# Opening of a decoder-layer kernel: two small loads issued by ScalarE instead of SyncE, and twelve idle products of TensorE split 6 + 8 instead of 8 + 4

## The reference, cut to what matters

```
h = concatenate([meta_tokens, x], axis=1)          # 272 x 2048
xn = rmsnorm(h, norm1_g)                           # h * rsqrt(mean(h*h) + eps) * norm1_g
proj = xn @ w_in                                   # 2048 x (columns of all mixers and gates)
... three token mixers, gated merge, w_o, residual, MLP (w_up, conv, w_down), final rmsnorm
```

## Time and profile before

| | us |
|---|---|
| median of 3 runs | 1773.64 |
| lowest, highest | 1773.37, 1773.96 |
| the profiled execution, its own time | 1775.31 |
| its span (first to last instruction) | 1773.6 |
| TensorE busy in it | 1762.3 (99%) |
| mean granted clock of TensorE | 0.998 |

### The profile page before, as it was taken

How to read it: one execution, slowest core, us unless ns; L and a number is a source line. 1 busy time by engine, 2 the same in 40 slices (tenths; PEclk the granted TensorE clock), 3 DMA queues, 4 the chain that set the end, 5 groups by cost and what they waited for, 6 DMA issues and landing times.

```text
span 1773.6 us, 34047 instructions
## 1 busy us (share of the span) xinstructions
PE 1762.3 (99%) x13517; PEld 1698.4 (96%) x13517; DVE 1133.6 (64%) x1557; ACT 763.9 (43%) x942; POOL 160.3 (9%) x306
## 2 busy tenths in 40 slices
PE   9999999999999999999999999999999999999998
PEld 8999999999999999999999999999999999888886
DVE  6857757677575545555556587777777777544444
ACT  6634444354354444444444444444434343443433
POOL 3030030210300000000000033331000000000000
PEclk9999999999999999999999999999999999999999
DMA  8655556556455565666555566666556555655554
GB/s 229 171 156 158 169 153 172 157 151 177 138 164 181 171 187 175 189 189 190 177 172 184 189 200 193 195 189 187 182 181 189 179 178 180 227 185 189 189 188 132
DMA packets 304662, 317.48 MB, mean 179 GB/s; under 512 B 13769, under 2 KB 279501, under 8 KB 304461
## 3 DMA queue, kind: packets, MB, share of 16 engines
q1 hardware_dynamic: 296861, 311.01, 57.7%
q0 software_dynamic: 7296, 4.68, 1.4%
q10 hardware_dynamic: 432, 0.79, 0.1%
HBM read 311.10 MB, written 2.11 MB: 177 GB/s over the span
## 4 chain that ended last, share of the span: by engine, by line
PE 99%; DVE 0%; DMA 0%; ACT 0%; SPq 0%; issue 0%; ACTq 0%; DVEq 0%
PE ps L1368 27%; PE ps L1369 27%; PE ps L1370 27%; PE ps L1643 5%; PE ps L1642 5%; PE ps L1644 5%; PE ps L1479 1%; PE ps L1459 0%; DMA xb<-in_x_dram 0%; PE ps L1494 0%; PE ps L1535 0%; PE ps L1534 0%; PE ps L1504 0%; PE ps L1495 0%; DVE xl L889 0%; PE ps L1522 0%
## 5 line engine op out<-in xcount | busy, mean ns | idle before, releaser
L845 DVE TENSOR_TENSOR lo<-raw,hi 128x1024 fp32r<-128x1024 f32 x584 | 710.6, 1229 | 506.6 <-ACT hi L565 501.6
L1368 PE MATMUL ps<-xh,hi 128*128 128x258 f32 (+2 forms) x3328 | 947.1, 285 | 0.2 <-DVE xl L889 0.2
L1369 PE MATMUL ps<-xl,hi 128*128 128x258 f32 (+2 forms) x3328 | 942.6, 283 | 0.0
L1370 PE MATMUL ps<-xh,lo 128*128 128x258 f32 (+2 forms) x3328 | 937.8, 282 | 0.0
L565 ACT CAST hi<-raw 128x1024 fp32r<-128x1024 f32 x584 | 604.5, 1048 | 679.6 <-PE ps L1370 544.6
L1368 PEld LDWEIGHTS ps<-xh,hi 128*128 128x128 f32 x3328 | 628.9, 189 | 1.4 <-issue 0.4
L1370 PEld LDWEIGHTS ps<-xh,lo 128*128 128x128 f32 x3328 | 629.7, 189 | 0.0
L1369 PEld LDWEIGHTS ps<-xl,hi 128*128 128x128 f32 x3328 | 628.2, 189 | 0.2
L1643 PE MATMUL ps<-hi,act_l 128*128 128x512 f32 x350 | 139.7, 399 | 0.0
L1642 PE MATMUL ps<-hi,act_h 128*128 128x512 f32 x350 | 137.9, 394 | 0.0
L1644 PE MATMUL ps<-lo,act_h 128*128 128x512 f32 x350 | 137.2, 392 | 0.0
(11 more groups left out here) (301 smaller groups left out, 1200.2 us busy)
## 6 DMA issues: line engine op xcount, KB each, us to landing
raw<-in_w_in_dram SPq DMA_DIRECT2D x224, 512.0 KB, 3.7
raw<-in_w_up_dram SPq DMA_DIRECT2D x176, 512.0 KB, 4.6
raw<-in_w_down_dram SPq DMA_DIRECT2D x88, 512.0 KB, 4.7
raw<-in_w_o_dram SPq DMA_DIRECT2D x32, 512.0 KB, 3.6
raw<-in_w_in_dram SPq DMA_DIRECT2D x32, 256.0 KB, 3.4
raw<-in_w_a_o_dram SPq DMA_DIRECT2D x16, 512.0 KB, 4.5
raw<-in_w_b_o_dram SPq DMA_DIRECT2D x16, 512.0 KB, 3.3
raw<-in_w_c_o_dram SPq DMA_DIRECT2D x16, 512.0 KB, 3.3
```

The costliest lines, as they stand in the source:

```text
L845: nc.vector.tensor_tensor(lo[:, s, :], raw[:, s, :], hi[:, s, :].bitcast(F32), ALU.subtract).then_inc(lo_ready, 1)
L1368: nc.tensor.matmul(acc, w_hi, mh, start=first and j == 0, stop=False)
L1369: nc.tensor.matmul(acc, w_hi, ml, start=False, stop=False)
L1370: ins = nc.tensor.matmul(acc, w_lo, mh, start=False, stop=last and j == KJ - 1)
```

## The change

Two edits. First, the two small loads (norm row and meta tokens) leave SyncE's program and become the first instructions of ScalarE's, in front of its table load. Second, of TensorE's idle products, the group of eight in front of chunk 1's transposes becomes six, and the group of four behind them becomes eight: twelve become fourteen. Nothing that is computed changes.

```diff
@@ SyncE
             load_input(0)
-            sp.dma_start(prow[0:KT, 4, :], norm1_g[0].rearrange("(a b) -> a b", b=P)).then_inc(g1_in, 16)
-            sp.dma_start(xa[:], meta_tokens.rearrange("m (c n) -> c m n", n=XC)).then_inc(xa_in, 16)
-
             def load(ph, i, q, w, k0, col):
@@ ScalarE
             def pair_done(ph, i, q):
                 act.wait_ge(panel_used, ph.panel(i, q) + 1)
 
+            act.dma_start(prow[0:KT, 4, :], norm1_g[0].rearrange("(a b) -> a b", b=P)).then_inc(g1_in, 16)
+            act.dma_start(xa[:], meta_tokens.rearrange("m (c n) -> c m n", n=XC)).then_inc(xa_in, 16)
             act.sem_inc(hi_ready, SLOTS)
@@ TensorE
             input_pair(1)
+            keep_warm(6, ident[:])
+            input_chunk(1)
             keep_warm(8, ident[:])
-            input_chunk(1)
-            keep_warm(4, ident[:])
```

## The result

| | kernel before | changed kernel |
|---|---|---|
| median of 14 runs, us | 1773.87 | 1776.97 |
| lowest, highest, us | 1773.37, 1774.13 | 1775.62, 1778.97 |
| traced execution, us (span) | 1775.31 (1773.6) | 1776.96 (1775.0) |

The changed kernel is 3.1 us slower: ratio 1.0018, 95% interval 1.0010 to 1.0026. The prediction said 1771.7, in a range of 1770.4 to 1773.9. It was wrong in sign and outside the range. The spread also grew, from 0.8 to 3.4 us.

The account below looks back on a forecast made before the run. TensorE, busy 99%, was taken as the bound, with only its opening waits and clock to change: 1.24 (earlier landing) - 0.89 (idle products) + 1.57 (clock) = 1.92 us off the median 1773.64, giving 1771.7, range 1770.4 to 1773.9.

Parts of the forecast that it names:

- Part 1: SyncE's queue: without the two small issues, panel 0 and chunk 1 are issued sooner; chunk 1 lands 1.24 us earlier.
- my lower end: Chunk 1's landing: only the DMA engines' empty time is filled, so it lands 1.04 us earlier.
- Part 2: ScalarE's queue: two issues before the table load hide in idle time, tokens no later unless the queue is slow; cost zero.
- R4: ScalarE's queue is late on its first transfer; over 0.2% slower needs tokens about 4 us later; 0.03 with the unforeseen.
- The sum: Whole opening: 1.24 (earlier landing) - 0.89 (more idle products) + 1.57 (clock) = 1.92 us gained.
- Part 3: TensorE's idle products: eight more records between chunk 1's transposes and panel 0 are paid in full, 0.89 us.
- Part 4: TensorE's clock in the opening stays high after a shorter empty time; gain 1.57 us, bounds 0 and 1.57, little confidence.
- the base: Starting time: the profiled execution, 1775.31, its 1.67 us above the runs' median taken as unchanged; median 1773.64.

Follow-up runs that it names:

- the second trace: The kernel before, unchanged, traced once more: this execution took 1774.10 us, with a span of 1772.4.
- the row form: The changed kernel with the meta tokens laid out by rows (partition = token x 8 + chunk), one block of 128 rows: 1773.74, ratio 0.9998.
- the first pause: The changed kernel, but SyncE waits behind chunk 0 until the meta tokens are there: 1775.91.

## Why the prediction was wrong, step by step

**Where the 3.1 us are.** The typical run of before is the second trace, 1774.10. Against it the changed kernel's trace, 1776.96, is 2.86 longer: 2.6 in the span and 0.26 outside it (1.96 against 1.70). Panel 0 starts at 14.68 instead of 12.17, 2.51 later:

| | us |
|---|---|
| late tokens: their transposes at 8.74 instead of 6.44 | +2.30 |
| wait for chunk 1, 1.16, gone | -1.16 |
| four more records between them and panel 0 (28 for 24), 4 x 0.112 | +0.45 |
| what is left: transposes and idle products at the low clock | +0.92 |

The low clock shows in the rows of that stretch as 1.17 us (tokens 0.49 for 0.42, second half of chunk 0 0.85 for 0.43, twelve records of idle products 2.02 for 1.34); the other rows differ by 0.25 the other way. From panel 0 to the span's end the two traces differ by another 0.1: TensorE waits 0.55 instead of 0.21 in front of panel 3, and about 0.2 of that comes back later at a place that I did not follow.

**Part 1 (SyncE, 1.24 us gained): right, and a little too small.** Chunk 1 was issued at 1.85 in the row form and its transposes began at 8.82, against 10.40 in the typical trace of before, 1.58 earlier; the bound from the issue alone was 1.44. From its issue to its landing it took 6.93 us (6.99 and 7.16 in the two traces of before), so it was simply moved, and the empty time of the DMA engines was not the limit that my lower end took it for. In the changed kernel itself TensorE came to chunk 1 only at 12.10 and did not wait, so no row shows its landing.

**Part 2 (ScalarE, cost nothing): this step failed.** I weighed how the tokens would delay chunk 0 (0 to 0.45 us; chunk 0's transposes came at 5.63, with a wait of 0.50) and never how chunk 0 and the panels would delay the tokens. "Not later unless the second queue is slow" put it at zero; it was 2.3 us. On SyncE's queue the order of issue protected the tokens: they had only chunk 0 and the norm row in front of them and were there at most 3.82 us after their issue, with panel 0 and chunk 1 issued right behind. On the second queue they share the DMA engines with all that the first one holds (4.56, 5.90 and 7.38 us as it held more), and it is just the other half of the edit that fills that one. R4 named the place and the lateness (a row of the tokens at 6.5 or later), but for another cause, a slow first transfer. The norm row alone, which cost nothing, and the 4.56 us of the first pause leave little to that one. R4 and the unforeseen together had 0.03. The sum gave the tokens the whole 288 GB/s of the stretch, 0.45 us, and asked only what chunk 0 loses; they got 7% of what was moved (last section).

**Part 3 (idle products, 0.89 on the path): right for the edit alone** (0.91 measured, no change inside the interval), wrong in its reason for the whole: with chunk 1 early the chain to `xl` is the limit, where the prediction had `xl` ready first, and 6 + 8 costs nothing against 8 + 4 (1773.74 and 1773.78).

**Part 4 and the base (clock, 1.57 gained): failed.** The traced execution lay 1.35 us above the slowest of the three runs beside it (1775.31 against 1773.96), whose own spread was 0.6, and I put that down as "the same before and after". It was the low clock itself, and the span was high with it: 1773.6, where the medians of the three sets of before have 1772.0 to 1772.2. The typical run had nothing to give back. Without this term the sum would have been 0.35 gained, 1773.5 from the 1773.87 of the 14 runs; with the tokens in rows the kernel runs at 1773.74, 0.02 under before in its set, so the gain shows in the trace (one-column product at 15.61 instead of 16.11) and hardly in the time. What tipped the prediction, that the clock fell behind the pause and not in it, does not hold either: in the changed kernel it fell 1.7 us into the wait for the tokens. The Trainium skill, page TensorE: Matmul & The Clock Gate, section Part 1: The HAM clock gate, says that the point of change varies with the start of a kernel. I set that aside on three runs; the two traces of the kernel before, one with the fall and one without, and the groups 1.6 us apart now agree with it.

**The whole.** The earlier landing of chunk 1 was right in mechanism and size. What failed is that one transfer moved to where it had no protection, and that one gain was taken from an untypical trace. 0.2 us remain that lie outside the span: time less span is 1.90 to 1.95 us on average in the five kernels here with the tokens on ScalarE's queue, besides 1.94 in the changed one, and 1.74 to 1.81 in the five with them on SyncE's. That is why the row form's shorter span on ScalarE's queue (median 1771.8, against 1772.0) gave no shorter time. What it is stays open.

## What to carry to other kernels

Moving a load to a second queue frees the first one's issue time but takes away the load's place in the line: from then on it shares the DMA engines with everything that the first queue issues, behind it as well. Move what is tiny (8 KB cost nothing here) or what nobody needs soon, and before moving anything look at the form of the transfer, which on the second queue was worth the whole loss. And before pricing an edit from one trace, compare that execution's time with the runs beside it: if it lies outside their spread, something in it is not typical.

## What the runs showed of the hardware that I had not expected

- Two queues did not share evenly by bytes here. From 2.5 to 8.7 us, while the 128 KB (131 thousand bytes) of the tokens were under way in the changed kernel, the DMA engines moved about 1.86 MB by the stretches of one microsecond (151, 278, 283, 341, 340, 301 and 341 GB/s): the tokens got 7%.
- The form of a transfer of 128 rows of 1 KB decides its issue (0.49 against 1.20 us on ScalarE, 0.41 against 0.79 on SyncE) and, on the queue that had SyncE's traffic beside it, its landing (5.2 and 5.55 against 7.07 and 7.38). On SyncE's own queue it did not: 4.3 and 4.4 against at most 3.82.
- Pauses of TensorE of 2.60 and 2.33 us (the pause behind chunk 0, the idle products alone) left the clock high in two executions, one of 1.94 us was followed by a fall in another, and the same kernel does either from run to run, 1.6 us apart.
- The column of the granted clock doesn't show the low level from the start: in the second trace of the changed kernel it reads 1.00 throughout, while products start at intervals of the low level until about 14 us:

```profile
12.00:13.00 1.00, 1.00 (x6) 1.00 (x6) 1.00 (x1) 1.00 (x4) 0.00 (x0) 1.00 1.11 367
```

Six records in a microsecond there stand against twelve in the same microsecond of the changed kernel's first trace. The 1.00 of the earlier trace rows is to be read with the same care: in that trace the first nine idle products, 18 records from 1.23 to 4.92, start 0.205 us apart, the interval of the low level. It changed no term of the prediction.
